# Expert weights of a mixture-of-experts trunk in wider column chunks: 35 units of two k tiles in place of 33

## The chip, the cores and the metric

The kernel runs on one core of a Trainium2 chip. The metric is the device time of one execution in microseconds. Before the change it is 1677.37 us, the median of three runs (1677.33 to 1680.08).

## The reference

Two layers over 256 tokens of width 1024, in float32: attention and a dense feed-forward in the first, a state-space mixer and a mixture of eight experts in the second. What the change touches is the mixture of experts:

```python
def moe_swiglu(h, w_router, wg, wu, wd):            # h: 256 tokens x 1024; wg, wu: 8 x 1024 x 2816; wd: 8 x 2816 x 1024
    logits = jnp.einsum('bsd,de->bse', h, w_router, preferred_element_type=jnp.float32)
    top_val, top_idx = lax.top_k(logits, TOP_K)     # 2 of 8 experts for each token
    gates = jax.nn.softmax(top_val, axis=-1)
    combine = jnp.sum(jax.nn.one_hot(top_idx, N_EXPERTS, dtype=jnp.float32) * gates[..., None], axis=-2)
...
        g = jnp.einsum('bqd,edf->bqef', hx, wg)
        u = jnp.einsum('bqd,edf->bqef', hx, wu)
        act = jax.nn.silu(g) * u * cx[..., None].astype(hx.dtype)
        return jnp.einsum('bqef,efd->bqd', act, wd)
```

## The kernel before

Float32 products are made of three matmuls: each operand is split into a rounded part (`hi`) and a remainder (`lo`), and hi x hi, hi x lo and lo x hi are added up in PSUM (`mm3`, lines 1279 to 1281). Every weight is split on the chip, the `hi` part by ScalarE (ACT, line 501), the `lo` part by VectorE (DVE, line 847).

The experts run as a loop of jobs, one expert for up to 128 chosen tokens; these inputs give 8 jobs (7 trips of the loop, and the last job written out behind it). For a job, TensorE (PE) first gathers its tokens with a selection matrix (`gather`, L1619, matmuls of 128 columns), then multiplies by gate and up weights, ACT applies silu (L788), DVE multiplies by up (`times_up`, L1224), PE turns the product (`turn`, L1675), ACT and DVE split it (`turn_hi` L793, `turn_lo` L1229), and PE multiplies by the down weights. The job's result is split (L820, L1257) and added to the token rows in the following job: `scatter(i)` on PE (L1642) puts one of four pieces into PSUM bank 7, `scatter_add(i)` on DVE (L1203) adds it to x. All four pieces use that one bank, so `scatter(i)` waits on the semaphore `sc_done` until `scatter_add(i-1)` is done.

Weights come in units of 1 MB (128 partitions x 2048 float32), 33 to a job, each by one DMA issued by SyncE (SP) into one of five slots. A slot's names in the profile are `ring`, `ring`, `ring`, `y`, `y` for the raw weights, `whi`, `whi`, `whi`, `hT_hi`, `st_hi` for the hi parts, and `wlo`, `wlo`, `hT_lo`, `elo`, `xn_lo` for the lo parts. Unit m goes through four steps in turn, and each frees what the next unit in the slot needs:

- SP issues its load when the lo part of the unit before it in the slot is made (`lo_ready`).
- ACT makes hi(m) when the load has landed and PE has used the slot's unit before (`units_used`).
- DVE makes lo(m) when hi(m) is there (`hi_ready`).
- PE uses it: 12 matmuls of 512 columns or 24 of 256.

Every engine takes its instructions strictly in the order in which they are written. On ACT and DVE `ahead_job(m)` writes out, at its place, all splits up to those for whose slot unit m must have been used. An operation behind `ahead_job(m)` therefore stands behind a split that waits for PE to use unit m.

gate and up are taken in six column chunks, five of 512 and one of 256. A unit of a chunk of 512 has four k tiles in rows of 2 KB; the units of the last chunk have eight k tiles in rows of 1 KB. The down weights come in ten units of four k tiles and half of the columns (rows of 2 KB) and one of two k tiles and all columns. On PE `scatter(0)` stands behind unit 5, `scatter(1)` behind unit 6 and one `turn`, `scatter(2)` behind `down(0, 0)`, and `scatter(3)` two gate units after `down(0, 1)`.

Near a job's end PE gathers the next job's tokens: `gather(0)` and `gather(1)` into banks 7 and 0, then `down(4, 0)`, which waits for `e_tlo`, set by `turn_lo(4)` on DVE.

Of the kernel before, what the change touches and what calls it, by code (L numbers as in the profile page):

```python
# [57 lines left out]
GATHER_BANK = (7, 0, 1, 7)  # L58
FCJ = 6
UJ = 33  # L60
SLOTS = P
OVER = 3
SLOT_GROUPS = (ES, ES, ES - 1, ES, ES - 1, ES, ES)
assert sum(SLOT_GROUPS) == UJ
# [67 lines left out]


def job_unit(c, part):

    gate = 0 if c == 0 else 4 + 6 * (c - 1)
    if part == 2:
        return UJ - 1 if c == FCJ - 1 else 30 if c == FCJ - 2 else 8 + 6 * c
    return gate + part * (1 if c == FCJ - 1 else 2)


def slot(m):

    for g in SLOT_GROUPS:
        if m < g:
            return m
        m -= g


def slot_before(m):  # L150

    return max(u for u in range(-UJ, m) if slot(u % UJ) == slot(m))


def slot_uses(i, m):

    return sum(1 for u in range(m) if slot(u) == i)


def trunk(nc, a, out):  # L160
# [5 lines left out]
    with ctx:  # L166
# [98 lines left out]
        aT_hi, aT_lo = (c[:, 12:16, :].rearrange("p (a k) (b s) -> p a (k b) s", a=2, b=2) for c in (cat_hi, cat_lo))  # L265
# [43 lines left out]
        def parts(n, kind):  # L309

            k = {"a": 8, "b": 4, "d": 2, "t": 8}[kind]
            w = 8 * NH if kind == "t" else UNIT
            pair = (whi[:, n % HIS, 0:w], wlo[:, n % LOS, 0:w]) if n < MOE else (ehi[slot(n - MOE)], elo[slot(n - MOE)])
            return tuple(v.rearrange("p (k c) -> p k c", k=k) for v in pair)

# [6 lines left out]
        def expert_landed(eng, m, job):  # L322
            i = slot(m)
            eng.wait_ge(expert_in[i], 16 * (slot_uses(i, m) + 1) + job * (16 * slot_uses(i, UJ)))
# [40 lines left out]
        def _(sp):  # L365
# [32 lines left out]
            def expert_loads(job, e):  # L398
                def w(name):
                    return a[name][0, bass.ds(e, 1)].rearrange("e (t p) n -> p (e t) n", p=P)  # L400
                srcs = [None] * UJ
                for part, name in enumerate(("moe_w_gate", "moe_w_up")):
                    for c in range(FCJ - 1):
                        for kg in range(2):
                            srcs[job_unit(c, part) + kg] = (w(name)[:, 4 * kg:4 * kg + 4, 512 * c:512 * c + 512], "b")
                    srcs[job_unit(FCJ - 1, part)] = (w(name)[:, :, 512 * (FCJ - 1):FF], "a")
                for c in range(FCJ - 1):
                    for n in range(2):
                        srcs[job_unit(c, 2) + n] = (w("moe_w_down")[:, 4 * c:4 * c + 4, 512 * n:512 * n + 512], "b")
                srcs[job_unit(FCJ - 1, 2)] = (w("moe_w_down")[:, 20:22, :], "d")  # L410
                for m, (src, kind) in enumerate(srcs):
                    k = {"a": 8, "b": 4, "d": 2}[kind]
                    sp.wait_ge(q["lo_ready"], MOE + slot_before(m) + 1 + job * UJ)
                    sp.dma_start(eraw[slot(m)].rearrange("p (k c) -> p k c", k=k), src).then_inc(expert_in[slot(m)], 16)
# [73 lines left out]
        def _(ac):  # L488
# [9 lines left out]
            def expert_hi(m, job):  # L498
                expert_landed(ac, m, job)
                ac.wait_ge(q["units_used"], MOE + slot_before(m) + 1 + job * UJ)  # L500
                nc.scalar.activation(ehi[slot(m)], eraw[slot(m)], ACT.Copy).then_inc(q["hi_ready"], 1)  # L501
# [266 lines left out]
            def expert(job, last):  # L768
                done = [ES]

                def ahead_job(m):

                    while done[0] < UJ + ES and (slot_before(done[0]) if done[0] < UJ else UJ + slot_before(done[0] - UJ)) <= m:
                        if done[0] < UJ:
                            expert_hi(done[0], job)
                        elif not last:
                            expert_hi(done[0] - UJ, job + 1)
                        done[0] += 1
# [4 lines left out]
                def silu(c):  # L783
                    w = 512 if c < FCJ - 1 else 256
                    m = job_unit(c, 0) + (1 if c < FCJ - 1 else 0)
                    ahead_job(m - 1)
                    used(m)
                    nc.scalar.activation(actf[:, c % 2, 0:w], PB[2 * (c % 2)][:, 0:w], ACT.Silu).then_inc(q["e_silu"], 1)  # L788

                def turn_hi(c):  # L790
                    nk = 4 if c < FCJ - 1 else 2
                    ac.wait_ge(q["e_t"], FCJ * job + c + 1)
                    nc.scalar.activation(aT_hi[:, c % 2, 0:nk, :], PB[4][:, 0:P * nk].rearrange("p (k s) -> p k s", k=nk), ACT.Copy).then_inc(q["e_thi"], 1)  # L793

                silu(0)
                silu(1)
                turn_hi(0)
                for c in range(2, FCJ - 1):
                    silu(c)
                    turn_hi(c - 1)  # L800
                    if c == 2:
                        ahead_job(job_unit(1, 2))
                        ac.wait_ge(q["selT_full"], job + 1)
                        nc.scalar.activation(selT, PB[7][:, 0:S].rearrange("p (t s) -> p t s", t=NT), ACT.Copy).then_inc(q["selT_done"], 1)
                silu(FCJ - 1)
                turn_hi(FCJ - 2)
                ahead_job(29)
                if not last:
                    gather_out(job + 1, 0)
                    gather_out(job + 1, 1)  # L810
                ahead_job(30)
                turn_hi(FCJ - 1)
                if not last:
                    gather_out(job + 1, 2)
                    ahead_job(31)
                    gather_out(job + 1, 3)
                ahead_job(31)
                used(UJ - 1)
                for n in range(2):
                    nc.scalar.activation(y_hi[:, 512 * n:512 * n + 512], PB[5 + n][:, :], ACT.Copy).then_inc(q["yhi_done"], 1)  # L820
                ahead_job(32)
# [11 lines left out]
        def _(ve):  # L833
# [10 lines left out]
            def expert_lo(m, job):  # L844

                ve.wait_ge(q["hi_ready"], MOE + m + 1 + job * UJ)
                ve.tensor_tensor(elo[slot(m)], eraw[slot(m)], ehi[slot(m)].bitcast(F32), ALU.subtract).then_inc(q["lo_ready"], 1)  # L847
# [358 lines left out]
            def expert(job, last):  # L1206
                done = [ES]

                def ahead_job(m):

                    while done[0] < UJ + ES and (slot_before(done[0]) if done[0] < UJ else UJ + slot_before(done[0] - UJ)) <= m:
# [6 lines left out]
                def times_up(c):  # L1218
                    w = 512 if c < FCJ - 1 else 256
                    m = job_unit(c, 1) + (1 if c < FCJ - 1 else 0)  # L1220
                    ahead_job(m - 1)
                    ve.wait_ge(q["units_used"], MOE + m + 1 + job * UJ)
                    ve.wait_ge(q["e_silu"], FCJ * job + c + 1)
                    ve.tensor_tensor(actf[:, c % 2, 0:w], actf[:, c % 2, 0:w], PB[2 * (c % 2) + 1][:, 0:w], ALU.mult).then_inc(q["e_act"], 1)  # L1224

                def turn_lo(c):
                    nk = 4 if c < FCJ - 1 else 2
                    ve.wait_ge(q["e_thi"], FCJ * job + c + 1)
                    ve.tensor_tensor(aT_lo[:, c % 2, 0:nk, :], PB[4][:, 0:P * nk].rearrange("p (k s) -> p k s", k=nk),  # L1229
                                     aT_hi[:, c % 2, 0:nk, :].bitcast(F32), ALU.subtract).then_inc(q["e_tlo"], 1)  # L1230
# [8 lines left out]
                ahead_job(job_unit(0, 2))  # L1239
                scatter_add(job, 2)  # L1240
                for c in range(2, FCJ - 1):
                    ahead_job(job_unit(c, 0))
                    if c == 2:
                        scatter_add(job, 3)
                    turn_lo(c - 1)
                    if c == 3 and not last:
                        choose(job + 1)
                    times_up(c)
                ahead_job(28)
                turn_lo(FCJ - 2)  # L1250
                times_up(FCJ - 1)
                ahead_job(30)
                turn_lo(FCJ - 1)
                ahead_job(31)
# [4 lines left out]
                ahead_job(32)  # L1259
# [14 lines left out]
        def _(pe):  # L1274
# [351 lines left out]
            for i in range(4):  # L1626
                if i == 3:
                    pe.wait_ge(q["ga_done"], 1)
# [19 lines left out]
            def expert(job, last_one):  # L1648
                def rows(c, part):

                    bank = PB[2 * (c % 2) + part]
                    if c >= 2 and part == 0:
                        pe.wait_ge(q["e_act"], FCJ * job + c - 1)
                    m = job_unit(c, part)
                    if c == FCJ - 1:
                        split_ready(MOE + m, job)
                        w = parts(MOE + m, "a")
                        for k in range(KD):
                            last = mm3(bank[:, 0:256], cut(xg, ALL, k), cut(w, ALL, k), k == 0, k == KD - 1)
                        last.then_inc(q["units_used"], 1)  # L1660
                    for kg in range(0 if c == FCJ - 1 else 2):
                        split_ready(MOE + m + kg, job)
# [124 lines left out]
```

## Time and profile before

| | |
|---|---|
| Median of 3 runs | 1677.37 us |
| The profiled execution | 1680.51 us, its span 1678.7 us |
| Span taken by the experts | from about 849 us to the end |
| PE busy over the span | 1561.9 us (93%) |
| DVE, ACT busy over the span | 1122.6 us (67%), 951.7 us (57%) |
| Read from HBM | 389.86 MB |

The page's busy time of PE is that of pipelined matmuls whose ends are modelled; a PE that reads 99% busy can still lose time when its clock is low or its matmuls start further apart. Starts are exact, so the distance between starts is what is used for times on PE. PEclk is the clock granted to TensorE as a share of 2.4 GHz: 0.50 is 1.2 GHz.

### The profile page before, as it was taken

The page shows a single profiled execution, that of the slowest core. Times are in us where ns is not written, and L with a number is a line of the kernel's source. Part 1 is how long each engine was busy: PE and PEld are TensorE (multiplying, and loading weights), DVE is VectorE, ACT ScalarE, POOL GpSimd, SP SyncE. Part 2 cuts the span into 40 slices and gives each one's busy share as a digit, 9 for nine tenths or more (in the row PEclk, how much of TensorE's full clock was granted, in tenths as well). Part 3 has the DMA queues.
Part 4 walks back from the last instruction along what each step waited for, and adds up shares of the span by engine and source line. Part 5 has one row for each costly group of instructions (what it writes and reads, how often), then busy time and mean ns, then how long its engine had stood idle before and what let it go on. Part 6 is the DMA issues. An engine that isn't in the chain of part 4 may idle for free.

```text
span 1678.7 us, 22515 instructions
## 1 busy us (share of the span) xinstructions
PE 1561.9 (93%) x8652; PEld 1357.4 (81%) x8652; DVE 1122.6 (67%) x997; ACT 951.7 (57%) x959; POOL 64.2 (4%) x85
## 2 busy tenths in 40 slices
PE   6999999999998768969599999999999999999996
PEld 6998899999897757858478788888888888888885
DVE  4455454444646655444498788797978978788885
ACT  5444453434546432433356777777677776777763
POOL 1000000000100026000000000000000000000000
PEclk9999999999999979979689999999999999999998
DMA  8433355656543420425479999999998999989992
GB/s 268 150 102 126 124 177 178 197 178 191 181 134 101 126 76 1 151 75 176 150 253 344 324 326 373 319 350 332 332 371 310 349 341 333 355 314 365 328 346 111
DMA packets 229602, 391.88 MB, mean 233 GB/s; under 512 B 7280, under 2 KB 82208, under 8 KB 229536
## 3 DMA queue, kind: packets, MB, share of 16 engines
q1 hardware_dynamic: 229536, 390.96, 67.2%
q8 instruction: 46, 0.75, 0.2%
q14 instruction: 20, 0.16, 0.0%
HBM read 389.86 MB, written 1.07 MB: 233 GB/s over the span
## 4 chain that ended last, share of the span: by engine, by line
PE 74%; DVE 8%; DMA 6%; issue 5%; ACT 5%; POOL 0%; SPq 0%; ACTq 0%; DVEq 0%; POOLq 0%
PE PB L1279 22%; PE PB L1280 21%; PE PB L1281 21%; DMA y<-in_moe_w_down 4%; DVE cv L1052 2%; ACT whi L496 1%; PE PB L1642 1%; DVE xn_lo L847 1%; PE PB L1619 1%; DMA ring<-in_moe_w_gate 1%; PE PB L1298 1%; PE PB L1570 1%; ACT whi L501 1%; ACT hT_hi L501 1%; PE PB L1361 1%
## 5 line engine op out<-in xcount | busy, mean ns | idle before, releaser
L1279 PE MATMUL PB<-whi,cat_hi 128*128 128x512 f32 (+1 forms) x1048 | 405.9, 387 | 14.4 <-DVE cat_lo L1229 11.5
L501 ACT ACTIVATE whi<-ring 128x2048 fp32r<-128x2048 f32 x168 | 321.0, 1916 | 142.6 <-PE PB L1281 118.2
L1281 PE MATMUL PB<-whi,cat_lo 128*128 128x512 f32 (+1 forms) x1048 | 399.1, 381 | 0.0
L841 DVE TENSOR_TENSOR wlo<-ring,whi 128x2048 fp32r<-128x2048 f32 (+1 forms) x103 | 234.1, 2273 | 205.4 <-PE PB L1281 171.4
L1280 PE MATMUL PB<-wlo,cat_hi 128*128 128x512 f32 (+1 forms) x824 | 309.0, 375 | 0.0
L847 DVE TENSOR_TENSOR wlo<-ring,whi 128x2048 fp32r<-128x2048 f32 x112 | 255.5, 2288 | 66.8 <-ACT whi L501 66.7
L1279 PEld LDWEIGHTS PB<-whi,cat_hi 128*128 128x128 f32 x1048 | 200.2, 191 | 51.5 <-DVE wlo L847 11.3
L1281 PEld LDWEIGHTS PB<-whi,cat_lo 128*128 128x128 f32 x1048 | 199.9, 191 | 37.7
L496 ACT ACTIVATE whi<-ring 128x2048 fp32r<-128x2048 f32 (+1 forms) x103 | 195.4, 1899 | 52.2 <-PE PB L1281 41.3
L1279 PE MATMUL PB<-hT_hi,whi 128*128 128x256 f32 x744 | 215.8, 290 | 2.7 <-DVE hT_lo L869 1.8
L1280 PE MATMUL PB<-hT_lo,whi 128*128 128x256 f32 x744 | 212.9, 286 | 0.0
L1281 PE MATMUL PB<-hT_hi,wlo 128*128 128x256 f32 x744 | 212.8, 286 | 0.0
L1280 PEld LDWEIGHTS PB<-wlo,cat_hi 128*128 128x128 f32 x824 | 156.4, 190 | 26.2
L1279 PEld LDWEIGHTS PB<-hT_hi,whi 128*128 128x128 f32 x744 | 145.6, 196 | 3.8 <-DVE hT_lo L869 2.2
L847 DVE TENSOR_TENSOR hT_lo<-ring,whi 128x2048 fp32r<-128x2048 f32 x56 | 128.2, 2288 | 28.9 <-ACT whi L501 28.9
L1280 PEld LDWEIGHTS PB<-hT_lo,whi 128*128 128x128 f32 x744 | 145.4, 195 | 0.5
L1281 PEld LDWEIGHTS PB<-hT_hi,wlo 128*128 128x128 f32 x744 | 145.1, 195 | 0.0
L847 DVE TENSOR_TENSOR elo<-y,hT_hi 128x2048 fp32r<-128x2048 f32 x56 | 128.2, 2289 | 16.5 <-ACT hT_hi L501 16.1
L501 ACT ACTIVATE hT_hi<-y 128x2048 fp32r<-128x2048 f32 x56 | 107.4, 1918 | 37.2 <-PE PB L1281 31.0
L847 DVE TENSOR_TENSOR xn_lo<-y,st_hi 128x2048 fp32r<-128x2048 f32 x40 | 91.5, 2288 | 10.9 <-ACT st_hi L501 10.9
L1280 PE MATMUL PB<-hT_lo,cat_hi 128*128 128x512 f32 x224 | 90.2, 403 | 0.0
L1279 PE MATMUL PB<-hT_hi,cat_hi 128*128 128x512 f32 x224 | 88.7, 396 | 0.0
(248 smaller groups left out, 2215.1 us busy)
## 6 DMA issues: line engine op xcount, KB each, us to landing
ring<-in_moe_w_gate SPq DMA_DIRECT2D x64, 1024.0 KB, 6.8
ring<-in_moe_w_up SPq DMA_DIRECT2D x64, 1024.0 KB, 7.4
y<-in_moe_w_down SPq DMA_DIRECT2D x48, 1024.0 KB, 8.0
ring<-in_moe_w_down SPq DMA_DIRECT2D x40, 1024.0 KB, 5.7
ring<-in_ssm_w_in SPq DMA_DIRECT2D x24, 1024.0 KB, 5.3
y<-in_moe_w_up SPq DMA_DIRECT2D x24, 1024.0 KB, 8.1
y<-in_moe_w_gate SPq DMA_DIRECT2D x24, 1024.0 KB, 6.8
ring<-in_w_mem_kv SPq DMA_DIRECT2D x16, 1024.0 KB, 5.4
```

The source lines that it names most:

```text
L496: nc.scalar.activation(whi[:, n % HIS, 0:w], ring[:, n % RING, 0:w], ACT.Copy).then_inc(q["hi_ready"], 1)
L501: nc.scalar.activation(ehi[slot(m)], eraw[slot(m)], ACT.Copy).then_inc(q["hi_ready"], 1)
L841: ve.tensor_tensor(wlo[:, n % LOS, 0:w], ring[:, n % RING, 0:w], whi[:, n % HIS, 0:w].bitcast(F32), ALU.subtract).then_inc(q["lo_ready"], 1)
L847: ve.tensor_tensor(elo[slot(m)], eraw[slot(m)], ehi[slot(m)].bitcast(F32), ALU.subtract).then_inc(q["lo_ready"], 1)
L1052: i = ve.scalar_tensor_tensor(out=cv[:, k, :], in0=u[:, tap:tap + S], scalar=w[:, tap:tap + 1], in1=cv[:, k, :], op0=ALU.mult, op1=ALU.add)
L1279: mm(out, lhs[0], rhs[0], start=start, stop=False)
L1280: mm(out, lhs[0], rhs[1], start=False, stop=False)
L1281: return mm(out, lhs[1], rhs[0], start=False, stop=stop)
L1298: last = nc.tensor.transpose(PB[4 + f % 2][:, S * i + P * t:S * i + P * t + P], src[:, t, P * (2 * g + i):P * (2 * g + i) + P], ident)
L1361: last = mm(bank[:, S * j:S * j + S], xqT[:, 2 * h + k, P * j:P * j + P], memK[:, 2 * h + k, :], start=k == 0, stop=k == 1)
L1570: last = mm(PB[4 + n % 2][:, P * h:P * h + P], Lm[:, n % 2, h, :], tri, start=True, stop=True)
L1619: last = mm(PB[GATHER_BANK[i]][:, P * k:P * k + P], src[:, t, P * (4 * (i % 2) + k):P * (4 * (i % 2) + k) + P], sel[:, t, :], start=t == 0 ...
```

## The change

The experts alone are changed. gate and up are taken in three column chunks of 1024, 1024 and 768. A unit has two k tiles, and its rows are 4 KB (3 KB in the third chunk). The down units have two k tiles and all 1024 columns. That makes 35 units a job: 27 of 1 MB and 8 of 0.75 MB. They go round the five slots by number (m % 5). The numbers of the first units of each chunk are in `GATE`, `UP` and `DOWN`. A chunk of gate takes PSUM banks 0 and 1, a chunk of up banks 2 and 3, and the gathers take banks 0 to 3. The products of a chunk are turned in two halves `turn(c, 0)` and `turn(c, 1)`. The order of the work on PE, ACT and DVE is written anew. The amount of matmul, split and copy work is the same, except that two more splits are made for the same number of elements.

```diff
-GATHER_BANK = (7, 0, 1, 7)
-FCJ = 6
-UJ = 33
+GATHER_BANK = (0, 1, 2, 3)
+CHUNKS = (1024, 1024, 768)
+GATE, UP, DOWN = (0, 8, 20), (4, 12, 24), (16, 28, 32)
+DOWNS = (4, 4, 3)
+UJ = 35
...
@@ sync
+                for m, src in enumerate(srcs):
+                    sp.wait_ge(q["lo_ready"], MOE + m - ES + 1 + job * UJ)
+                    dst = eraw[m % ES][:, 0:2 * job_width(m)].rearrange("p (k c) -> p k c", k=2)
+                    sp.dma_start(dst, src).then_inc(expert_in[m % ES], 16)
...
@@ scalar
                 def ahead_job(m):
-                    while done[0] < UJ + ES and (slot_before(done[0]) if done[0] < UJ else UJ + slot_before(done[0] - UJ)) <= m:
+                    while done[0] <= m + ES:
...
+                def silu(c):
+                    ahead_job(GATE[c] + 2)
+                    used(GATE[c] + 3)
+                    if c:
+                        ac.wait_ge(q["e_t"], 6 * job + 2 * c)
+                    for h in range(2):
+                        w = min(512, CHUNKS[c] - 512 * h)
+                        last = nc.scalar.activation(actf[:, h, 0:w], PB[h][:, 0:w], ACT.Silu)
+                    last.then_inc(q["e_silu"], 1)
...
                 silu(0)
+                ahead_job(8)
...
@@ vector
+                def times_up(c):
+                    ahead_job(UP[c] + 3)
+                    ve.wait_ge(q["units_used"], MOE + UP[c] + 4 + job * UJ)
+                    ve.wait_ge(q["e_silu"], 3 * job + c + 1)
...
+                for i in range(4):
+                    ahead_job(3 + i)
+                    scatter_add(job, i)
                 times_up(0)
-                ahead_job(4)
-                scatter_add(job, 0)
-                turn_lo(0)
-                ahead_job(5)
-                scatter_add(job, 1)
...
@@ tensor
+                for kg in range(4):
+                    gate(0, kg)
+                for kg in range(4):
+                    scatter(job, kg)
+                    up(0, kg)
+                gate(1, 0)
+                pe.wait_ge(q["sc_done"], 4 * job + 4)
...
+                for kg in range(4):
+                    up(2, kg)
+                down(1, 0)
                 if not last_one:
...
                     gather(job + 1, 0)
-                    pe.wait_ge(q["e_act"], FCJ * job + c)
                     gather(job + 1, 1)
+                down(1, 1)
+                turn(2, 0)
+                down(1, 2)
```

On DVE, at the start of a job. Before: the third split of the job is followed by `times_up(0)`, and two more splits stand ahead of the first `scatter_add` (L1203), with one further split between the first two of them.

```order
L847 TENSOR_TENSOR hT_lo<-ring,whi 128x2048 [waits hi_ready]
L1222 REGISTER_ALU
L1223 ISA [waits units_used]
L1224 TENSOR_TENSOR actf<-actf,PB 128x512 [waits e_silu]
L846 REGISTER_ALU
L847 TENSOR_TENSOR elo<-y,hT_hi 128x2048 [waits hi_ready]
L846 REGISTER_ALU
L847 TENSOR_TENSOR xn_lo<-y,st_hi 128x2048 [waits hi_ready]
L1201 ISA
L1203 REGISTER_ALU [waits sc_full]
L1203 SCALAR_TENSOR_TENSOR x<-PB,jobcomb,x 128x512
```

After, the same place (L834 is the lo split, L1190 `scatter_add`). The `elo` row is the split of unit 8, `xn_lo` that of unit 9:

```order
L834 TENSOR_TENSOR hT_lo<-ring,whi 128x2048 [waits hi_ready]
L832 REGISTER_ALU
L834 TENSOR_TENSOR elo<-y,hT_hi 128x2048 [waits hi_ready]
L1188 ISA
L1190 REGISTER_ALU [waits sc_full]
L1190 SCALAR_TENSOR_TENSOR x<-PB,jobcomb,x 128x512
L832 REGISTER_ALU
L834 TENSOR_TENSOR xn_lo<-y,st_hi 128x2048 [waits hi_ready]
L1188 REGISTER_ALU
L1190 SCALAR_TENSOR_TENSOR x<-PB,jobcomb,x 128x512 [waits sc_full]
```

What moved: `times_up(0)` went behind all four `scatter_add`s, and each `scatter_add(i)` now stands right behind the split of unit 8 + i, which waits (through hi) for PE to use unit 3 + i.

On PE, `scatter(1)` (L1642 before, L1627 after). Before it stands behind unit 6, whose slot is 1 (`whi`, `wlo`):

```order
L1279 MATMUL PB<-whi,cat_hi 128x512
L1280 MATMUL PB<-wlo,cat_hi 128x512
L1281 MATMUL PB<-whi,cat_lo 128x512
L1637 REGISTER_ALU
L1642 MATMUL PB<-cat_hi 128x512 [waits sc_done]
L1642 MATMUL PB<-cat_lo,cat_hi 128x512
L1306 REGISTER_ALU
L1279 MATMUL PB<-whi,cat_hi 128x512 [waits lo_ready]
```

After, it stands behind unit 4 (`st_hi`, `xn_lo`), which is `up(0, 0)`:

```order
L1266 MATMUL PB<-st_hi,cat_hi 128x512
L1267 MATMUL PB<-xn_lo,cat_hi 128x512
L1268 MATMUL PB<-st_hi,cat_lo 128x512
L1622 REGISTER_ALU
L1627 MATMUL PB<-cat_hi 128x512 [waits sc_done]
L1627 MATMUL PB<-cat_lo,cat_hi 128x512
L1293 REGISTER_ALU
L1266 MATMUL PB<-whi,cat_hi 128x512 [waits lo_ready]
```

What moved: the four scatters, which stood at units 6, 7, 9 and 12 of the job, stand one unit apart ahead of units 4, 5, 6 and 7.

## Rows read from the trace of the kernel before

**Rows 1.** Page, part 1: busy us, share of the span, instructions.
```profile
PE 1561.9 (93%) x8652; PEld 1357.4 (81%) x8652; DVE 1122.6 (67%) x997; ACT 951.7 (57%) x959; POOL 64.2 (4%) x85
```
**Rows 2.** Windows, jobs: us, busy PE, PEld, DVE, ACT, POOL, PEclk, DMA, GB/s.
```profile
972.50:1073.00 100.50, 99.49 (x485) 83.06 (x485) 85.03 (x54) 74.02 (x54) 0.00 (x0) 1.00 0.96 344
...
1378.90:1481.80 102.90, 101.01 (x485) 84.21 (x484) 85.25 (x54) 74.23 (x54) 0.00 (x0) 0.98 0.94 336
```
**Rows 3.** Waits, 870 to 1678 us: waiting op <- releaser: total us, times, longest.
```profile
ACT whi L501 <- DMA ring<-in_moe_w_down: 12.0, 15, 1.6
PE PB L1279 <- DVE cat_lo L1229: 11.5, 8, 3.0
```
**Rows 4.** Timeline, PE, two job ends: start us, us, operation, count [idle before <-releaser].
```profile
942.87 0.77 PE L1279 MATMUL PB<-whi,cat_hi 128*128 128x512 f32 x1 [2.96 <-DVE cat_lo L1229]
...
1043.06 1.90 PE L1619 MATMUL PB<-cat_hi 128*128 128x128 f32 x16
1045.86 0.47 PE L1279 MATMUL PB<-whi,cat_hi 128*128 128x512 f32 x1 [0.90 <-DVE cat_lo L1229]
...
1249.36 0.77 PE L1279 MATMUL PB<-whi,cat_hi 128*128 128x512 f32 x1 [1.71 <-DVE cat_lo L1229]
```
**Rows 5.** Windows behind such waits.
```profile
941.90:948.70 6.80, 5.83 (x16) 4.59 (x16) 3.35 (x4) 1.88 (x4) 0.00 (x0) 0.50 1.06 384
...
1146.70:1150.10 3.40, 3.40 (x9) 2.67 (x9) 2.14 (x1) 0.36 (x1) 0.00 (x0) 0.50 1.05 386
...
1249.10:1252.50 3.40, 3.14 (x8) 2.50 (x9) 2.64 (x3) 0.85 (x2) 0.00 (x0) 0.50 1.05 386
1453.90:1457.30 3.40, 3.40 (x10) 2.63 (x9) 1.54 (x1) 0.00 (x0) 0.00 (x0) 0.50 1.05 386
```
**Rows 6.** Timeline, PE, around scatters 0 and 1.
```profile
972.10 0.39 PE L1281 MATMUL PB<-whi,cat_lo 128*128 128x512 f32 x1
...
973.45 0.39 PE L1280 MATMUL PB<-wlo,cat_hi 128*128 128x512 f32 x1
...
975.74 0.39 PE L1281 MATMUL PB<-whi,cat_lo 128*128 128x512 f32 x1
976.22 0.50 PE L1642 MATMUL PB<-cat_hi 128*128 128x512 f32 x1
976.56 0.40 PE L1642 MATMUL PB<-cat_lo,cat_hi 128*128 128x512 f32 x1
```
**Rows 7.** Timeline, ACT: start us, us.
```profile
960.35 1.92 ACT L501 ACTIVATE whi<-ring 128x2048 fp32r<-128x2048 f32 x1
962.28 1.28 ACT L788 ACT_TABLE_LOAD   x1
963.58 0.60 ACT L788 ACTIVATE actf<-PB 128x512 f32<-128x512 f32 x1
964.07 3.71 ACT L501 ACTIVATE whi<-ring 128x2048 fp32r<-128x2048 f32 x2
...
972.52 0.60 ACT L788 ACTIVATE actf<-PB 128x512 f32<-128x512 f32 x1 [0.80 <-PE PB L1281]
...
1040.87 1.91 ACT L501 ACTIVATE whi<-ring 128x2048 fp32r<-128x2048 f32 x1
```
**Rows 8.** Timeline, DVE.
```profile
973.22 2.28 DVE L847 TENSOR_TENSOR xn_lo<-y,st_hi 128x2048 fp32r<-128x2048 f32 x1
975.43 0.74 DVE L1203 SCALAR_TENSOR_TENSOR x<-PB,jobcomb,x 128x512 f32<-128x512 f32 x1
976.09 0.68 DVE L1229 TENSOR_TENSOR cat_lo<-PB,cat_hi 128x512 fp32r<-128x512 f32 x1
...
1042.82 2.29 DVE L847 TENSOR_TENSOR wlo<-ring,whi 128x2048 fp32r<-128x2048 f32 x1 [0.91 <-ACT whi L501]
1045.02 0.69 DVE L1229 TENSOR_TENSOR cat_lo<-PB,cat_hi 128x512 fp32r<-128x512 f32 x1
```
**Rows 9.** DMA queue, 960 to 1560 us: packets, MB, share of 16 engines.
```profile
q1 hardware_dynamic: 107480, 204.31, 95.5%
```

More of the change, by code:

```diff
@@ L131, in ffn_at @@
     return max(3 * c - 1, 0) + part
[L134 to L157, printed above, removed]
 def trunk(nc, a, out):
@@ L795, in expert @@
-                silu(0)
-                silu(1)
[L797 to L805, printed above, removed]
@@ L808, in expert @@
+                silu(2)
+                ahead_job(28)
                 if not last:
@@ new lines, in expert @@
+                for i in range(4):
+                    ahead_job(3 + i)
+                    scatter_add(job, i)
+                times_up(0)
+                ahead_job(9)
+                turn_lo(0, 0)
+                ahead_job(10)
+                turn_lo(0, 1)
+                times_up(1)
+                ahead_job(17)
+                if not last:
+                    choose(job + 1)
+                ahead_job(19)
+                turn_lo(1, 0)
+                ahead_job(20)
+                turn_lo(1, 1)
@@ L1249, in expert @@
+                times_up(2)
                 ahead_job(28)
[L1250 to L1251 removed]
+                turn_lo(2, 0)
                 ahead_job(30)
[L1253 to L1254 removed]
+                turn_lo(2, 1)
+                ahead_job(33)
                 for n in range(2):
@@ L1648, in expert @@
             def expert(job, last_one):
[L1649 to L1662, printed above, removed]
-                        w = parts(MOE + m + kg, "b")
-                        for k in range(4):
-                            last = mm3(bank[:, :], cut(xg, ALL, 4 * kg + k), cut(w, ALL, k), kg == 0 and k == 0, kg == 1 and k == 3)
-                        last.then_inc(q["units_used"], 1)
-                        yield kg
@@ L1669, in turn, with rows @@
-                def turn(c):
-                    nk = 4 if c < FCJ - 1 else 2
-                    pe.wait_ge(q["e_act"], FCJ * job + c + 1)
-                    if c:
-                        pe.wait_ge(q["e_tlo"], FCJ * job + c)
+                def rows(at, c, banks, m):
+                    split_ready(MOE + m, job)
+                    w = job_parts(m)
+                    kg = m - at[c]
+                    for k in range(2):
+                        for h in range(2):
+                            n = min(512, CHUNKS[c] - 512 * h)
+                            last = mm3(PB[banks + h][:, 0:n], cut(xg, ALL, 2 * kg + k), cut(w, ALL, k, slice(512 * h, 512 * h + n)),
+                                       kg == 0 and k == 0, kg == 3 and k == 1)
+                    last.then_inc(q["units_used"], 1)
@@ new lines, in gate, with up, turn @@
+                def gate(c, kg):
+                    if c and kg == 0:
+                        pe.wait_ge(q["e_silu"], 3 * job + c)
+                    rows(GATE, c, 0, GATE[c] + kg)
+                def up(c, kg):
+                    if c and kg == 0:
+                        pe.wait_ge(q["e_act"], 3 * job + c)
+                    rows(UP, c, 2, UP[c] + kg)
+                def turn(c, h):
+                    nk = min(4, CHUNKS[c] // P - 4 * h)
+                    pe.wait_ge(q["e_act"], 3 * job + c + 1)
+                    if c or h:
+                        pe.wait_ge(q["e_tlo"], 6 * job + 2 * c + h)
@@ L1686, in down @@
                     last.then_inc(q["units_used"], 1)
                 pe.wait_ge(q["ga_done"], 4 * job + 4)
-                for _ in rows(0, 0):
-                    pass
-                for _ in rows(0, 1):
-                    pass
-                for _ in rows(1, 0):
-                    pass
-                scatter(job, 0)
-                turn(0)
-                for kg in rows(1, 1):
-                    if kg == 0:
-                        scatter(job, 1)
-                down(0, 0)
@@ L1701, in expert @@
-                scatter(job, 2)
-                down(0, 1)
-                for c in range(2, FCJ - 1):
-                    for _ in rows(c, 0):
-                        pass
-                    if c == 2:
-                        scatter(job, 3)
-                    turn(c - 1)
-                    for _ in rows(c, 1):
-                        pass
-                    down(c - 1, 0)
-                    if c == 2:
-                        pe.wait_ge(q["sc_done"], 4 * job + 4)
-                        for t in range(NT):
-                            last = nc.tensor.transpose(PB[7][:, P * t:P * t + P], sel[:, t, :].bitcast(F32), ident)
-                        last.then_inc(q["selT_full"], 1)
-                    down(c - 1, 1)
@@ L1718, in expert @@
-                c = FCJ - 1
-                for _ in rows(c, 0):
-                    pass
-                turn(c - 1)
-                for _ in rows(c, 1):
-                    pass
+                for kg in range(4):
[5 more added lines that the diff above has]
+                pe.wait_ge(q["sc_done"], 4 * job + 4)
+                for t in range(NT):
+                    last = nc.tensor.transpose(PB[7][:, P * t:P * t + P], sel[:, t, :].bitcast(F32), ident)
@@ new lines, in expert @@
+                last.then_inc(q["selT_full"], 1)
+                gate(1, 1)
+                gate(1, 2)
+                turn(0, 0)
+                gate(1, 3)
+                turn(0, 1)
+                for kg in range(4):
+                    up(1, kg)
+                for kg in range(4):
+                    down(0, kg)
+                gate(2, 0)
+                turn(1, 0)
+                gate(2, 1)
+                turn(1, 1)
+                gate(2, 2)
+                gate(2, 3)
+                for kg in range(4):
+                    up(2, kg)
```

145 lines of the change are left out of this document (63 added, 82 removed).

## The prediction

> **What bounds the kernel now.** I read the page first, then the stretch of the experts by windows, the waits, and the timelines of PE, ACT and DVE at the places where PE stops. The page has PE at 93% of the span, DVE at 67%, ACT at 57% [rows 1]. In the experts both PE and the DMA engines look full: in a job of 100.5 to 102.9 us PE is busy for all but 1 to 2 us and the DMA share is 0.94 to 0.96 [rows 2, 9]. The waits tell the two apart. No matmul waits for a DMA. What PE waits for is `turn_lo` on DVE, once near the end of each of the 8 jobs, 11.5 us in all [rows 3]. A late load shows only on ACT, 12.0 us in 15 waits in the largest such group [rows 3], most of it covered. So PE bounds the experts, DMA comes close behind, and a job holds about 99 us of PE work: 100.5 us less the 1.2 us at its end.
>
> Two things besides the work cost PE time. Behind the wait at the job's end the granted clock sometimes falls to 0.50, which is 1.2 GHz: for 6.8 us after the wait of 2.96 us, for 3.4 us in three more jobs, among them the one with 1.71 us, and not at all after the wait of 0.90 us [rows 4, 5]. And `scatter(1)` starts 0.48 us after the matmul before it instead of 0.23, since `scatter_add(0)` has only just ended on DVE [rows 6, 8].
>
> **Matmuls, splits, copies.** PE has the same matmuls, gathers, scatters and transposes a job as before; ACT and DVE split the same number of elements in two more instructions. They have the room: DVE is busy 85 of 100.5 us, ACT 74 [rows 2]. I take 0 for this, on the ground that PE waits for them only at the places treated below.
>
> **DMA.** The rows of a unit grow from 2 KB (1 KB in two of the units) to 4 and 3 KB, with the same bytes in all. No row of before isolates such packets. If a byte costs what it costs now, a job's loads take 0.96 x 100.5 = 96.5 us of the 16 engines [rows 2]; that is one bound, and less is the other. Either lies under the 99 us of PE work, so what the change saves here is hidden by PE. It does make the late loads rarer that lengthen the wait at the job's end. The Trainium skill speaks for more: "Perfetto Trace Analysis", section DMA Optimizations, says that DMAs under 2 KB pay much overhead for each transfer, and that batching them from 2 KB to 4 or 8 KB can improve throughput dramatically where the kernel is bound by DMA. The share of 0.96 fits the condition, the waits of PE do not; by the rule the change would be a gain. It has its case among the rivals.
>
> **The end of a job (removed).** Now PE comes to `down(4, 0)` right behind two gathers and waits for `turn_lo(4)`. After the change a down unit stands between each gather pair and turn, and `down(2, 0)` waits for a `turn_lo(2, 0)` that is two down units and two gathers old. I take the whole wait as gone: 11.5 us [rows 3]. With it goes the clock at half: 6.8 + 3 x 3.4 = 17 us at half speed, 8 us after taking off the part in which PE waited anyway [rows 4, 5]. The small wait of `scatter(1)` goes as well, about 2 us in 8 jobs [rows 6]. Together 21.5 us. What is late next there is `turn(2, 0)`, which needs `times_up(2)`: ACT and DVE must first split unit 32, whose slot is freed by unit 27. ACT makes hi(28) to hi(32) at 1.9 us each while PE takes the narrow units 23 to 27 at 2.1 us each; by adding the durations of rows 7 and 8 I get the product 6.8 us after PE's unit 27 and PE at `turn(2, 0)` after 7.2 us (one unit of 2.75, sixteen gather matmuls in 1.7 [rows 4], another unit). That cover is 0.4 us thin; I take 0, and up to 1 us a job if it fails.
>
> **The start of a job (added).** Here the order does harm. `scatter_add(0)` stands behind the split of unit 8, and that waits until PE has used unit 3, the last before `scatter(0)`. PE has only `up(0, 0)` to do before `scatter(1)`, which waits for `scatter_add(0)`. Zero is the start of unit 3's last matmul.
> - ACT sees a used unit 0.42 us after the start of its last matmul (972.10 to 972.52) [rows 6, 7]. hi(7) starts by that at -2.3 us, a unit of 12 matmuls being 2.75 us (ten steps in 2.29 us) [rows 6], and ends at -0.4. The table load, which ACT takes once a job ahead of `silu(0)`, ends 1.28 us later, at 0.90 [rows 7].
> - The two silu start at 0.92 and 1.41, as the next instruction starts 0.49 us behind one of 512 columns (963.58 to 964.07) [rows 7]. hi(8) starts at 1.90 and ends at 3.82.
> - lo(8) starts at 3.86 (1040.87 + 1.91 to 1042.82) [rows 7, 8], `scatter_add(0)` 2.21 us behind it, at 6.07, and ends at 6.81; PE starts 0.05 us after that (976.17 to 976.22), at 6.86 [rows 6, 8].
> - PE would be there at 0.23 + 0.46 for `scatter(0)` + 2.75 for `up(0, 0)` = 3.44. The wait is 3.4 us, and the first matmul behind it costs 0.1 more (0.34 instead of 0.23) [rows 6].
>
> `scatter(2)` does not wait: hi(9), lo(9) and `scatter_add(1)` end at 9.68, `up(0, 1)` at 10.18. `scatter(3)` does. The last matmul of `up(0, 1)` starts at 9.95; hi(10) runs from 10.37 to 12.28, lo(10) from 12.32, `scatter_add(2)` from 14.53 to 15.27. PE is there at 10.18 + 0.46 + 2.75 = 13.39 and starts at 15.32: 1.9 us, and 0.1 for the restart. Behind `up(0, 3)` the same chain brings `times_up(0)` to its end 5.8 us later, while PE has three gate units (8.3 us) before `turn(0, 0)`: covered by 2.5 us.
>
> Sum: 3.4 + 0.1 + 1.9 + 0.1 = 5.5 us a job, 44 us in 8 jobs. What would hide it is nothing on PE: these four units and scatters are all that stands there, in order.
>
> **The clock behind the new waits.** A wait of 3.4 us in dense work has the one of 2.96 us as its nearest row: 6.8 us at half speed, 3.4 us lost, 2.9 of it outside the wait. The rows of 1.7 us cost 1.7 us, the one of 0.90 us nothing [rows 4, 5]. So a job loses between 0 and 2.9 + 1.7 = 4.6 us. At half speed `up(0, 1)` and `up(0, 2)` take longer, which eats up some of the second wait. I take 1.5 us for the first wait and 0.5 for the second: 2 us a job, 16 in all, between 0 and 37.
>
> **The sum.** 1680.5 us of the profiled execution + 44 + 16 - 21.5 = 1719. That execution is 3.1 us above the median of the runs shown, 1677.4, so I forecast 1716 us.
>
> **Rivals.**
> - *The clock holds.* The waits come, but a fall of the clock costs nothing beyond them, or the slow matmuls eat up the second wait in each job. Then 1716 - 16 = 1700. For it: after 0.90 us the clock held [rows 4, 5]. Against it: both longer waits shown lowered it.
> - *Faster, by DMA.* Loads set the pace at the job's end, through ACT and DVE, and at the start of a job DVE is further ahead than I think, so that no scatter waits. Then only the removed part counts: 1677.4 - 21.5 = 1656; below that the 99 us of PE work a job do not let it go. This is also what the rule of the skill gives here. For it: DMA share 0.94 to 0.96, and late loads on ACT [rows 2, 3]. Against it: the wait for `used(3)` is written into the order, and faster loads do not shorten it.
> - *Slower still.* Both new waits cost the full clock price of the rows, 4.6 us a job, or the thin cover at `turn(2, 0)` fails in each job: 1716 + 21 = 1737 by the first, 1724 by the second. It decides from the point where the clock stays at 0.50 over more than 3.4 us a job.
> - *Nothing moves.* The new waits come to 2.7 us a job in place of 7.5, just the 21.5 us that go: 1677. It needs a shorter chain on ACT and DVE than the rows show.
>
> **Chances.** The forecast 0.60 (its own range 1708 to 1729), the clock holds 0.16, faster 0.12, slower still 0.08, nothing moves 0.04. The range 1690 to 1740 leaves out the two cases at or below 1677 and little above. Within 0.2%, or 3.4 us, a time cannot be told from no change. Slower 0.85, within 0.2% 0.03, faster 0.12.
>
> **What would show it.** Right: in each job the first matmul of `scatter(1)` and of `scatter(3)` waits for DVE's `scatter_add` by 3.4 and 1.9 us; PEclk at 0.50 behind them in most jobs; no wait for `turn_lo` at a job's end; DMA share under 0.9 with time to spare; jobs of 105 to 108 us. Wrong: scatters that wait under 1 us each, or matmuls of the experts that start under 0.22 us apart, which would mean that loads had been slowing PE itself.

## The result, and the profile after

| | median us | runs | ratio to the kernel before (95% interval) |
|---|---|---|---|
| before | 1677.35 | 1676.79 to 1680.08 (4) | |
| the change | 1724.31 | 1717.26 to 1728.87 (4) | 1.0273 (1.0236 to 1.031) |

The change makes the kernel 2.7% slower. The forecast was 1716 us, in a range of 1690 to 1740. The profiled execution took 1724.95 us, its span is 1723.1 us, 44.4 us above that of before.

The page of the changed kernel answers to [rows 1]: the same 8652 matmuls, and little more on ACT and DVE (16 instructions each, for two more units in 8 jobs).

```profile
PE 1578.9 (92%) x8652; PEld 1366.8 (79%) x8652; DVE 1125.4 (65%) x1013; ACT 953.1 (55%) x975; POOL 65.1 (4%) x85
```

The waits from 870 to 1640 us (columns as in [rows 3]; the first job's first wait and the last job's end lie outside). The wait for `turn_lo` (`cat_lo`) is gone, and PE waits for `scatter_add` (L1190) 15 times instead, 16 times with the one that lies outside: twice in each job.

```profile
PE PB L1627 <- DVE x L1190: 36.7, 15, 3.2
```

Two jobs by windows, against [rows 2]. A job went from 100.5 to 102.9 us to 107.3 to 107.7 us; DMA share and GB/s fell, PEclk is below 1 in both.

```profile
970.60:1078.30 107.70, 102.63 (x486) 85.12 (x484) 85.58 (x55) 74.23 (x57) 0.00 (x0) 0.97 0.88 321
1078.30:1185.60 107.30, 102.26 (x486) 84.92 (x484) 85.57 (x55) 74.23 (x57) 0.00 (x0) 0.97 0.89 323
```

PE at the start of the second job, against [rows 6] (L1627 is `scatter`):

```profile
970.51 0.39 PE L1268 MATMUL PB<-st_hi,cat_lo 128*128 128x512 f32 x1
974.14 0.50 PE L1627 MATMUL PB<-cat_hi 128*128 128x512 f32 x1 [3.25 <-DVE x L1190]
974.48 0.39 PE L1627 MATMUL PB<-cat_lo,cat_hi 128*128 128x512 f32 x1
...
982.01 0.39 PE L1268 MATMUL PB<-whi,cat_lo 128*128 128x512 f32 x1
984.21 0.50 PE L1627 MATMUL PB<-cat_hi 128*128 128x512 f32 x1 [1.82 <-DVE x L1190]
```

From start to start the two waits are 974.14 - 970.51 = 3.63 and 2.20 us; less the 0.23 us that a matmul takes, 3.40 and 1.97. So it is in every job (3.40 and 3.41, and 1.95 to 1.97), but for the first wait of the eighth, 2.95 us: there no table load stands ahead of silu on ACT. The chain behind the first, on ACT and on DVE, against [rows 7, 8]:

```profile
968.21 1.09 ACT L769 ACTIVATE actf<-PB 128x512 f32<-128x512 f32 x2
969.19 1.92 ACT L480 ACTIVATE hT_hi<-y 128x2048 fp32r<-128x2048 f32 x1
```

```profile
971.13 2.29 DVE L834 TENSOR_TENSOR elo<-y,hT_hi 128x2048 fp32r<-128x2048 f32 x1 [1.47 <-ACT hT_hi L480]
973.34 0.74 DVE L1190 SCALAR_TENSOR_TENSOR x<-PB,jobcomb,x 128x512 f32<-128x512 f32 x1
```

The last matmul of unit 3 started 3.21 us before that of `up(0, 0)`, at 967.30. From there hi(8) starts at 1.89, lo(8) at 3.83, `scatter_add(0)` at 6.04 and `scatter(1)` at 6.84; the prediction had 1.90, 3.86, 6.07 and 6.86.

The granted clock behind the waits, against [rows 5]:

```profile
975.30:978.70 3.40, 3.40 (x10) 2.65 (x9) 1.65 (x2) 0.00 (x0) 0.00 (x0) 0.50 1.01 383
985.50:988.90 3.40, 3.40 (x10) 2.63 (x9) 1.83 (x2) 0.00 (x0) 0.00 (x0) 0.51 0.90 329
1081.10:1087.90 6.80, 6.01 (x14) 4.81 (x15) 3.59 (x4) 0.00 (x0) 0.00 (x0) 0.50 0.99 373
```

Such stretches stand behind a wait in every one of the 8 jobs: one or two of 3.4 us, or one of 6.8 us with or without one of 3.4 us. They add up to 51 us in the 8 jobs, 6.4 us a job, against 17 us before.

### The profile page after: what moved, and what is told of

The parts are those of the page before. It is cut to its first block, busy times and chain, and to the rows that moved or that the text cites. A ratio compares the mean times of both kernels' runs of the same rounds, so it can differ in the third digit from the quotient of the medians.

```text
span 1723.1 us, 22637 instructions
## 1 busy us (share of the span) xinstructions
PE 1578.9 (92%) x8652; PEld 1366.8 (79%) x8652; DVE 1125.4 (65%) x1013; ACT 953.1 (55%) x975; POOL 65.1 (4%) x85
## 4 chain that ended last, share of the span: by engine, by line
PE 80%; DVE 7%; ACT 6%; issue 5%; DMA 1%; POOL 0%; SPq 0%; DVEq 0%; ACTq 0%; POOLq 0%
PE PB L1266 23%; PE PB L1267 23%; PE PB L1268 23%; PE PB L1606 2%; DVE cv L1039 2%; ACT whi L480 1%; ACT whi L474 1%; PE PB L1662 1%; PE PB L1627 1%; PE PB L1285 1%; DVE x L1190 1%; PE PB L1557 1%; ACT hT_hi L480 1%; PE PB L1348 1%; DVE nt L1063 1%
## 5 line engine op out<-in xcount | busy, mean ns | idle before, releaser
L1266 PE MATMUL PB<-whi,cat_hi 128*128 128x512 f32 x984 | 391.3, 398 | 2.8 <-DVE cat_lo L856 1.8
L480 ACT ACTIVATE whi<-ring 128x2048 fp32r<-128x2048 f32 (+1 forms) x168 | 299.7, 1795 | 160.3 <-PE PB L1268 154.7
L1268 PE MATMUL PB<-whi,cat_lo 128*128 128x512 f32 x984 | 382.9, 389 | 0.0
L827 DVE TENSOR_TENSOR wlo<-ring,whi 128x2048 fp32r<-128x2048 f32 (+1 forms) x103 | 233.9, 2272 | 206.3 <-PE PB L1268 174.2
L1267 PE MATMUL PB<-wlo,cat_hi 128*128 128x512 f32 x760 | 296.9, 391 | 0.0
L834 DVE TENSOR_TENSOR wlo<-ring,whi 128x2048 fp32r<-128x2048 f32 (+1 forms) x112 | 238.1, 2136 | 70.7 <-ACT whi L480 70.6
L474 ACT ACTIVATE whi<-ring 128x2048 fp32r<-128x2048 f32 (+1 forms) x103 | 195.4, 1899 | 54.0 <-PE PB L1268 42.5
L834 DVE TENSOR_TENSOR elo<-y,hT_hi 128x2048 fp32r<-128x2048 f32 (+1 forms) x56 | 123.9, 2213 | 32.9 <-ACT hT_hi L480 32.7
L834 DVE TENSOR_TENSOR hT_lo<-ring,whi 128x2048 fp32r<-128x2048 f32 (+1 forms) x56 | 119.6, 2136 | 33.3 <-ACT whi L480 32.6
L834 DVE TENSOR_TENSOR xn_lo<-y,st_hi 128x2048 fp32r<-128x2048 f32 (+1 forms) x56 | 123.9, 2212 | 10.6 <-ACT st_hi L480 9.1
L480 ACT ACTIVATE hT_hi<-y 128x2048 fp32r<-128x2048 f32 (+1 forms) x56 | 104.0, 1857 | 38.0 <-PE PB L1268 27.1
L480 ACT ACTIVATE st_hi<-y 128x2048 fp32r<-128x2048 f32 (+1 forms) x56 | 103.9, 1855 | 28.7 <-PE PB L1268 27.9
```

What stands on the lines that cost most here:

```text
L474: nc.scalar.activation(whi[:, n % HIS, 0:w], ring[:, n % RING, 0:w], ACT.Copy).then_inc(q["hi_ready"], 1)
L480: nc.scalar.activation(ehi[m % ES][:, 0:w], eraw[m % ES][:, 0:w], ACT.Copy).then_inc(q["hi_ready"], 1)
L827: ve.tensor_tensor(wlo[:, n % LOS, 0:w], ring[:, n % RING, 0:w], whi[:, n % HIS, 0:w].bitcast(F32), ALU.subtract).then_inc(q["lo_ready"], 1)
L834: ve.tensor_tensor(elo[m % ES][:, 0:w], eraw[m % ES][:, 0:w], ehi[m % ES][:, 0:w].bitcast(F32), ALU.subtract).then_inc(q["lo_ready"], 1)
L1266: mm(out, lhs[0], rhs[0], start=start, stop=False)
L1267: mm(out, lhs[0], rhs[1], start=False, stop=False)
```

## The experiments

Each edit is against the changed kernel unless it says otherwise. The runs of before beside them had medians of 1677.0 us (experiments 1 to 4) and 1677.8 us (5 to 8). "Ratio" is that to the kernel before, with its 95% interval.

**1. adds_first.** Undo the order of `scatter_add` on DVE alone.

```diff
                 for i in range(4):
-                    ahead_job(3 + i)
+                    ahead_job(2 + i)
                     scatter_add(job, i)
```

> The changed kernel, with each scatter_add(i) on DVE one split earlier: behind the split of unit 7 + i instead of unit 8 + i. Nothing else moves. My theory (the two waits of 3.4 and 2.0 us a job, and the clock at half behind them, are the whole loss): scatter(1) and scatter(3) wait under 0.3 us, the granted clock stays at 1.0 in nearly all of the experts, and the time falls by 44 us of waits and some 22 us of clock to 1657 us (1650 to 1665), below the kernel before. Rival (the wait only moves on, because DVE splits one unit later than it did and PE then waits for a split or for times_up(0)): 1695 us or more, with a new wait for wlo, xn_lo or actf in each job. Rival (wider chunks or longer DMA rows cost time themselves): 1680 to 1700 us with no such wait.

Measured: 1660.96 us (1660.31 to 1661.98), ratio to before 0.9896 (0.9875 to 0.9917). One edit of an index takes 63 us off the changed kernel and puts it 1% below the kernel before. The windows of two jobs, and PE at the place where `scatter(2)` stands:

```profile
967.00:1066.40 99.40, 99.32 (x486) 82.94 (x484) 85.53 (x56) 74.31 (x56) 0.00 (x0) 1.00 0.96 348
1066.40:1165.60 99.20, 99.13 (x486) 82.91 (x484) 85.36 (x56) 74.29 (x56) 0.00 (x0) 1.00 0.95 347
```

```profile
966.99 0.39 PE L1268 MATMUL PB<-whi,cat_lo 128*128 128x512 f32 x1
967.46 0.50 PE L1627 MATMUL PB<-cat_hi 128*128 128x512 f32 x1
```

A job takes 99.2 to 99.4 us, the 99 us of PE work that the prediction read out of the kernel before, and the clock stays at 1.0 throughout the loop. What is left is 0.24 us at `scatter(2)` (0.47 instead of 0.23), in seven of the 8 jobs, and a wait of 1.0 us in the last job, ahead of `turn(2, 0)`. Neither rival holds: no wait for a split took the old one's place, and the wide chunks cost nothing by themselves.

**2. first_add_only.** The same for `scatter_add(0)` alone.

```diff
-                    ahead_job(3 + i)
+                    ahead_job(3 + i if i else 2)
```

> The changed kernel with scatter_add(0) alone one split earlier; the other three stay. My theory, by the same sum of durations: scatter(1) no longer waits; scatter_add(1) now stands behind lo(9), which ends 8.3 us after unit 3, and ends at 9.0, while PE is at scatter(2) after 6.6: one wait of 2.4 us a job, and scatter(3) waits no more. That saves 3.0 us a job, 24 us in all, and of the clock about half, 8 to 12 us: 1690 us (1683 to 1700). If the clock costs nothing by itself: 1700. If the first wait alone is the whole harm: 1670.

Measured: 1685.11 us (1683.71 to 1687.02), ratio 1.005 (1.0034 to 1.0067). The one wait is where and as long as computed, 2.66 us from start to start or 2.43 us of waiting:

```profile
972.76 0.80 PE L1627 MATMUL PB<-cat_hi 128*128 128x512 f32 x1 [2.27 <-DVE x L1190]
```

In the 8 jobs the clock is at 0.50 for 17 us, a third of the 51 us of the changed kernel. The time is 5 us below the figure expected, inside its range: I had put down that half of the clock's loss would stay.

**3. hi8_before_silu.** Shorten the chain on ACT: the split of unit 8 ahead of the table load and the two silu.

```diff
                 def silu(c):
-                    ahead_job(GATE[c] + 2)
+                    ahead_job(GATE[c] + (2 if c else 3))
```

> The changed kernel with ACT's split of unit 8 ahead of silu(0) instead of behind it, so that the table load and the two silu (1.5 us) leave the chain to scatter_add(0). My theory: scatter(1) waits 1.9 us instead of 3.4, but ACT then comes late to unit 9, so that scatter(2) waits about 0.9 and scatter(3) about 1.0: 3.9 us a job instead of 5.4, 12 us less in all, and with no wait over 2 us the clock falls less often, 5 to 15 us: 1703 us (1695 to 1712). Rival (the chain does not run over ACT, DVE alone is late): no change, 1720 to 1728.

Measured: 1700.68 us (1699.21 to 1704.7), ratio 1.0139 (1.0114 to 1.0165). The waits in the second job:

```profile
969.51 0.50 PE L1627 MATMUL PB<-cat_hi 128*128 128x512 f32 x1 [1.83 <-DVE x L1190]
...
973.71 0.50 PE L1627 MATMUL PB<-cat_hi 128*128 128x512 f32 x1 [0.71 <-DVE x L1190]
...
977.99 0.50 PE L1627 MATMUL PB<-cat_hi 128*128 128x512 f32 x1 [0.81 <-DVE x L1190]
```

By starts they are 1.99, 0.87 and 0.97 us, where 1.9, 0.9 and 1.0 were expected. Four of the 8 jobs show two waits of 1.9 to 2.0 us instead of three; in three of these the clock fell behind the first wait, and the slow matmuls took the place of the wait at `scatter(2)`. The chain does run over ACT, and the durations of before give its length.

**4. before_turn_lo_early.** On the kernel before: `turn_lo(4)` ahead of the split of the next job's unit 0.

```diff
-                ahead_job(28)
+                ahead_job(27)
                 turn_lo(FCJ - 2)
+                ahead_job(28)
                 times_up(FCJ - 1)
```

> The kernel before, with turn_lo(4) on DVE ahead of the split of the next job's unit 0 instead of behind it. It measures what the change really took away. My theory: the wait for turn_lo (11.5 us in 8 jobs) goes, and with it the clock at half (8 us): 1658 us (1653 to 1664). Rival (loads set the pace in the kernel before, DMA share 0.96, and PE waits elsewhere instead): 1668 to 1677 us.

Measured: 1662.54 us (1659.4 to 1663.94), ratio 0.9898 (0.9875 to 0.9921). The waits of PE from 860 to 1640 us and a job's window:

```profile
PE PB L1280 <- DVE cat_lo L1229: 1.9, 2, 1.7
```

```profile
971.40:1070.90 99.50, 99.38 (x486) 83.08 (x485) 85.33 (x54) 74.21 (x55) 0.00 (x0) 1.00 0.98 348
```

The kernel before was held up by its order on DVE at one place, not by its loads: with rows of 2 KB and a DMA share of 0.98 its job takes 99.5 us. Against adds_first that is 0.1 to 0.3 us a job. The new chunks, the longer rows and the four gather banks of the change together are worth no more than that; nearly all of its good lies in the wait at the job's end, and one line moved in the old kernel gets that too. One wait of 1.7 us for `turn_lo` is left, in the last job, which is part of why the time lies 4.5 us above the 1658 expected, though in its range.

**5. rows_2kb and 6. rows_4kb_two_dmas.** These two differ in the length of the rows. Both load each unit of adds_first by two DMAs and wait for 32 instead of 16; the first splits by columns, the second by k tile.

```diff
-                    sp.dma_start(dst, src).then_inc(expert_in[m % ES], 16)
+                    if job_width(m) == 1024:
+                        dst, n = dst.rearrange("p (h k c) -> p h k c", h=2, k=2), 512
+                        pairs = [(dst[:, h], src[:, :, n * h:n * h + n]) for h in range(2)]
...
+                    for to, at in pairs:
+                        sp.dma_start(to, at).then_inc(expert_in[m % ES], 16)
```

```diff
-                    sp.dma_start(dst, src).then_inc(expert_in[m % ES], 16)
+                    for k in range(2):
+                        sp.dma_start(dst[:, k], src[:, k]).then_inc(expert_in[m % ES], 16)
```

> The kernel of adds_first with each unit of weights loaded by two DMAs of half its size: the 27 units of 1 MB in rows of 2 KB, laid out in two column halves, the 8 of 0.75 MB in rows of 3 KB. Matmuls, splits and their order are the same. My theory (the length of the rows is hidden behind PE): the time of adds_first, 1661 us, to within 4 us, with a DMA share some hundredths higher or equal. Rival (the rows of 2 KB set the pace in the kernel before, and 4 KB are what makes adds_first faster than it): 1670 to 1680 us, and splits on ACT that wait for loads in every job.

> The kernel of adds_first with each unit loaded by two DMAs, one for each k tile, in rows of 4 KB (3 KB in the units of 0.75 MB). It is the partner of rows_2kb: the same number of DMAs, twice the length of row. My theory: 1661 us to within 4 us, as rows_2kb. Rival: rows_2kb is 10 us or more slower than this one; if both are slower than adds_first, it is the number of DMAs and not the rows.

Measured: 1663.30 us (1660.71 to 1665.54), ratio 0.9912 (0.9888 to 0.9935), with 2 KB; 1660.96 us (1659.85 to 1663.32), ratio 0.9902 (0.9879 to 0.9925), with 4 KB. The queue over 960 to 1560 us (columns as in [rows 9]), rows_2kb and then rows_4kb_two_dmas:

```profile
q1 hardware_dynamic: 102574, 208.84, 98.9%
```

```profile
q1 hardware_dynamic: 60882, 209.14, 95.8%
```

The same bytes take 98.9% of the engines in the shorter rows and 95.8% in the longer, 3% less. The time differs by 2.3 us and the intervals overlap, so a gain of that size is not shown, and one of 10 us is excluded. The traces do show a place where the shorter rows reach PE, in rows_2kb (L1676 is `turn`, L1220 `times_up`):

```profile
ACT whi L489 <- DMA ring<-in_moe_w_down: 14.3, 20, 1.3
PE PB L1676 <- DVE actf L1220: 2.8, 2, 2.3
```

In its last job the splits on ACT ahead of `times_up(2)` each wait some 0.8 us for their load. `turn(2, 0)` then waits 2.3 us, where in rows_4kb_two_dmas it waits 1.0, and the clock falls for 3.4 us behind it; one other job has a wait of 0.5 us there. By starts these come to 1.9 us, and the clock to 1.7, of the 4.2 us between the two profiled executions (1665.04 and 1660.80). So the rival's sign, splits that wait for loads, is there, 20 waits of 14.3 us against 8 of 4.4 us with the longer rows, but it costs PE time only at this one place. The rule of the Trainium skill on larger DMA sizes ("Perfetto Trace Analysis", DMA Optimizations) does not find its condition here: PE and not the queue is the bound, even at 98.9%. Two jobs of rows_2kb took 99.4 us each.

**7. waits_filled.** The price of the clock by itself: PE is kept busy in the two waits by matmuls that add nothing to the output.

```diff
                 for kg in range(4):
+                    for _ in range((0, 14, 0, 8)[kg]):
+                        mm(PB[4][:, :], selT[:, 0, :], y_hi[:, 0:512], start=True, stop=True)
                     scatter(job, kg)
                     up(0, kg)
```

> The changed kernel with 14 matmuls of 512 columns ahead of scatter(1) and 8 ahead of scatter(3) in each job, into PSUM bank 4, which nobody reads there; they add nothing to the output. They last 3.2 and 1.8 us and fill the two waits, so PE stays busy and the waits for scatter_add stay what they are in length. It measures the clock's price by itself. My theory: the granted clock stays at 1.0 in the experts, the time falls from 1724 by the part that the clock costs, 63 us of difference to adds_first less 43 of waits, about 20 us: 1704 us (1699 to 1709). Rival (the clock falls for other reasons, or the extra matmuls delay the chain): no change, or above 1720.

Measured: 1703.58 us (1702.11 to 1706.4), ratio 1.0155 (1.0131 to 1.0179). Two jobs:

```profile
965.00:1069.60 104.60, 104.52 (x508) 86.99 (x507) 85.64 (x56) 74.35 (x57) 0.00 (x0) 1.00 0.91 331
1069.60:1174.20 104.60, 104.52 (x508) 87.01 (x507) 85.65 (x56) 74.36 (x57) 0.00 (x0) 1.00 0.92 331
```

The delays keep their length. The matmul ahead of the 14 started at 968.85 us, so `scatter(1)` is 3.41 us late, and `scatter(3)` is 1.98 us late in the same way:

```profile
969.08 3.33 PE L1681 MATMUL PB<-cat_hi 128*128 128x512 f32 x14
972.49 0.50 PE L1627 MATMUL PB<-cat_hi 128*128 128x512 f32 x1
```

With PE busy through the same delay the clock stays at 1.0, and 1724.31 - 1703.58 = 20.7 us go. The rest, 1703.58 - 1660.96 = 42.6 us, is the two waits: 5.3 us a job, as against the 0.24 us at `scatter(2)` of adds_first. It is odd but true here that a kernel gets faster by 176 useless matmuls.

**8. tidy_end.** adds_first, with the last crumbs of waiting taken out.

```diff
                 for i in range(4):
-                    ahead_job(2 + i)
+                    ahead_job((2, 2, 3, 4)[i])
                     scatter_add(job, i)
...
                 down(1, 1)
-                turn(2, 0)
-                down(1, 2)
+                if last_one:
+                    down(1, 2)
+                    turn(2, 0)
+                else:
+                    turn(2, 0)
+                    down(1, 2)
```

> The kernel of adds_first with scatter_add(1) and scatter_add(2) and (3) one more split earlier on DVE, for the 0.23 us that scatter(2) still waits in each job, and in the last job turn(2, 0) behind down(1, 2) instead of ahead of it, for the 1.2 us that it waits for times_up(2) where no gathers stand ahead. Both theories expect little: 1.6 + 1.2 = 3 us less than adds_first, 1658 us; no change if the earlier scatter_adds only delay the splits.

Measured: 1656.73 us (1655.94 to 1659.15), ratio 0.9878 (0.9855 to 0.9901). It is the fastest of the kernels tried, 4 us below adds_first, and its profile shows no wait of PE for ACT or DVE between the first job's start and the last job's end. Two of its jobs took 99.0 us each. The two edits were measured together only.

## Why the prediction was right, point by point

| term, us | predicted | measured | from |
|---|---|---|---|
| the two new waits | +44 | +42.6 | waits_filled less adds_first |
| the clock behind them | +16 | +20.7 | the change less waits_filled |
| what the change removes | -21.5 | -16.4 | adds_first less before, 1660.96 - 1677.35 |
| sum | +38.5 | +46.9 | |

The measured terms are differences of medians of four kernels in a row, so they must add up to 1724.31 - 1677.35; what tests the prediction is each term by itself.

**What bounds the kernel.** Right. PE bounds the experts, and both kernels without waits come to 99.2 to 99.5 us a job, with rows of 2 or of 4 KB.

**The start of a job.** Right in place, cause and size. Every time of the first chain, worked out from rows of other places in the kernel before, came within 0.03 us, and the second wait came to 1.97 us for 1.93. The prediction took the table load as one in every job; the eighth has none there and waits 0.45 us less. Experiments 2 and 3 moved and shortened the chain, and the waits followed to 0.1 us.

**The clock.** Right in kind, too small by 4.7 us. I had put 2 us a job; it was 2.6. The first wait drew 3.4 or 6.8 us at half speed behind it in each job, and the second drew its own 3.4 us, 1.7 us lost, in four of 8, which is 0.85 us a job where I had put 0.5. The bound of 37 us held. One step was wrong: that the slow matmuls eat up some of the second wait. It is 1.95 to 1.96 us in the jobs with 6.8 us at half speed too (1093.15 - 1090.97 - 0.23 in the third), for the split that it waits for starts only when PE has used unit 5, and the slow matmuls delay that as well. The rows that the prediction went by were also the tidy ones: in the kernel before, a wait of 0.98 us was followed by 3.4 us at half clock ([rows 5], from 1146.70), and a longer one of 1.27 us by none, as the window in the third line shows (columns as in [rows 2]).

```profile
1146.45 0.55 PE L1279 MATMUL PB<-whi,cat_hi 128*128 128x512 f32 x1 [0.98 <-DVE cat_lo L1229]
1351.73 0.47 PE L1279 MATMUL PB<-whi,cat_hi 128*128 128x512 f32 x1 [1.27 <-DVE cat_lo L1229]
1351.50:1355.00 3.50, 3.27 (x17) 2.77 (x18) 2.62 (x3) 1.10 (x3) 0.00 (x0) 1.00 1.05 387
```

So the length of a wait alone does not tell whether the clock falls behind it, and that 16 us came so near to 20.7 is in part luck.

**The end of a job.** Right that the wait and its half clock would go; 5 us too much was put down. Three causes are seen. The rows were those of one execution that lay 3.1 us above its median and had 17 us at half clock, while the medians are compared here: by profiled spans the removal is 1678.7 - 1658.9 = 19.8 us. Then adds_first, by which the term is measured, has the 0.24 us at `scatter(2)`, and 0.1 us behind it, in seven jobs, 2.4 us in all. The changed kernel has not (0.23 us from start to start, at 979.05), so these belong to the waits and not to the removal; tidy_end, without them and without the wait named next, is 20.6 us below the kernel before. And in the last job the thin cover at `turn(2, 0)` did fail, since there are no gathers ahead of it there. In the changed kernel:

```profile
1692.63 0.65 PE L1662 MATMUL PB<-con,actf 128*128 128x128 f32 x4 [1.42 <-DVE actf L1211]
```

In the other seven jobs it held, 0.4 us or not. The prediction counted the gathers as work that stands in every job; in the last they don't.

**DMA.** Right that longer rows are hidden. The forecast of a share under 0.9 came true (0.88 and 0.89), but mainly for another reason than the rows: the jobs are longer. Without the waits the share is back at 0.95 to 0.96, the same as before with half as many packets. By experiments 5 and 6 rows of 4 KB freed about 3% of the engines here. Shorter rows reached PE at one place only, `turn(2, 0)`.

**The rivals.** *Faster, by DMA* fell with experiments 4 to 6: the gain of 1% lies in the order, and at most 2 us of it in the rows. *The clock holds* gave 1700; a kernel in which it does hold measures 1703.6. The waits alone make the change slower; of the 63 us between it and adds_first the clock is a third. *Slower still* named as its sign more than 3.4 us a job at 0.50. The sign came (6.4 us a job), its price of 4.6 us a job did not (2.6). Its other branch gave 1724, the very figure measured, but by a cover at `turn(2, 0)` that fails in each job, and it failed in one: the agreement is chance. *Nothing moves* asked for 2.7 us a job of new waits; they are 5.3.

The changed kernel and the one before spread most: 11.6 us over four runs and 13.0 us over eleven (1669.96 to 1682.92), against 1.7 us for adds_first. Both have waits behind which the clock falls at some and not at others. A varying number of falls would do this, and the mean granted clock of each run fits: in the runs of the change it is 0.955, 0.952, 0.950 and 0.948 for 1717.26, 1723.66, 1724.95 and 1728.87 us. A difference of 0.007 over 1720 us is 24 us more at half clock, 12 us lost. It was not tested by itself.

## What to carry to other kernels

An in-order engine that both feeds and drains another one needs its queue read item by item: a short operation that somebody waits for (here 0.74 us of `scatter_add`) must not stand behind a split that needs the waiter's own progress. Take the durations from the trace of before, put both queues side by side from the last common semaphore, and the wait can be computed to a tenth of a microsecond before anything is built. Count in what a fall of the clock behind the wait may cost; here that was half as much again as the waits. And look whether a change's gain is not to be had by moving one line of the old kernel.

## What was not expected of the hardware

- The seven waits of 2.43 us in first_add_only drew 3.4 us at half clock five times, the eight of 1.99 us in hi8_before_silu three times, and the eight of 0.9 to 1.0 us there never. In the kernel before one of 0.98 us did, and one of 1.27 us did not. Matmuls without use kept the clock at 2.4 GHz through 8 delays of 3.4 us.
- Doubling the rows from 2 to 4 KB cut the share of the DMA engines for the same bytes from 98.9 to 95.8%, no more (the 8 narrow units of a job had 3 KB in both).
- A DMA share of 0.99 over 600 us (rows_2kb) went together with PE at its full pace, 99.4 us a job. The share alone did not say what bounds.
